# One query projected earlier, the samples' squares in one block, and narrower waits ahead of the up-projection of a hybrid decoder layer

## What is computed

```
h  = rms_norm(x, norm2_g)
q  = rms_norm((h @ w_query).reshape(tokens, 8, 256), qnorm_g)
s1 = q[..., :128] . subkeys[:, 0]      s2 = q[..., 128:] . subkeys[:, 1]
v1, i1 = top_k(s1, 16)                 v2, i2 = top_k(s2, 16)
sc, ci = top_k(v1[:, None] + v2[None, :], 16)      e = (i1 * 128 + i2) at ci
g  = softmax(sc)
a  = gelu(h . u[e])
out = sum over the 8 * 16 chosen experts of g * a * v[e]
```

## Time and profile before

| | before |
|---|---|
| median of 3 runs | 1767.89 us |
| the profiled execution's own time | 1769.0 us |
| its span, from first to last instruction | 1767.2 us |
| PE busy | 1738.9 us (98%) |
| DVE busy | 1202.1 us (68%) |
| ACT busy | 557.6 us (32%) |
| POOL busy | 543.6 us (31%) |
| chain that ended last, by engine | PE 91%, DVE 6%, DMA 1%, issue 1%, ACT 1% |
| the same by line, the largest | L2149 39%, L2197 28%, L1829 17% |

### The profile page before, as it was taken

One profiled execution on the slowest core, in us unless ns is written; L12 is line 12 of the kernel. 1 busy time (PEld: TensorE's weight loads), 2 busy tenths in 40 slices (PEclk: granted clock), 3 DMA queues, 4 the chain that ended last, 5 costly groups with the idle time before them and its releaser, 6 DMA issues.

```text
span 1767.2 us, 30915 instructions
## 1 busy us (share of the span) xinstructions
PE 1738.9 (98%) x12653; PEld 1296.9 (73%) x12653; DVE 1202.1 (68%) x2475; ACT 557.6 (32%) x920; POOL 543.6 (31%) x586
## 2 busy tenths in 40 slices
PE   8999999999999999999999999999989999999999
PEld 7744446788888888888888888888746666666666
DVE  7659866759989948878265555545347667777764
ACT  2013246003242233544344444444212222222220
POOL 0000334022657602000000000000377777777760
PEclk9999999999999999999999999999989999999999
DMA  4431833031223444666998889775589999999991
GB/s 173 111 111 66 294 110 144 4 119 49 87 106 108 155 158 184 247 270 251 323 294 292 302 302 299 255 264 185 224 321 358 361 358 355 353 353 348 351 350 59
DMA packets 137486, 400.00 MB, mean 226 GB/s; under 512 B 13881, under 2 KB 86865, under 8 KB 125569
## 3 DMA queue, kind: packets, MB, share of 16 engines
q1 hardware_dynamic: 108816, 315.81, 48.2%
q0 software_dynamic: 28528, 82.22, 13.2%
HBM read 321.50 MB, written 76.46 MB: 225 GB/s over the span
## 4 chain that ended last, share of the span: by engine, by line
PE 91%; DVE 6%; DMA 1%; issue 1%; ACT 1%; SPq 0%; DVEq 0%; ACTq 0%
PE psum L2149 39%; PE psum L2197 28%; PE psum L1829 17%; PE psum L2170 2%; DMA qrow<-d_q 1%; PE psum L1844 1%; PE psum L2043 0%; PE psum L1964 0%; PE psum L1982 0%; DVE kprod L1239 0%; DVE sSc L1240 0%; PE psum L1881 0%; PE psum L1835 0%; ACT Pb L947 0%; PE psum L1933 0%
## 5 line engine op out<-in xcount | busy, mean ns | idle before, releaser
L2197 PE MATMUL psum<-w_hl,v_hi 128*128 128x376 bf16 x2048 | 493.1, 324 | 4.1 <-issue 4.1
L2149 PE MATMUL psum<-h_hi,u_hi 128*128 128x260 bf16 x2048 | 394.7, 274 | 0.7 <-ACT Ssb L1002 0.7
L2149 PE MATMUL psum<-h_lo,u_hi 128*128 128x260 bf16 x2048 | 394.4, 274 | 0.0
L2149 PE MATMUL psum<-h_hi,u_lo 128*128 128x260 bf16 x2048 | 394.2, 274 | 0.0
L822 POOL DMA_INDIRECT t_dots<-d_acts,t_lists x144 | 171.8, 1193 | 631.8 <-issue 631.8
L2197 PE MATMUL psum<-w_hl,v_lo 128*128 128x376 bf16 x1024 | 332.0, 324 | 3.4 <-issue 3.4
L2197 PEld LDWEIGHTS psum<-w_hl,v_hi 128*128 128x128 bf16 x2048 | 200.9, 98 | 134.5 <-issue 11.3
L1737 DVE TENSOR_TENSOR v_lo<-v_raw,v_hi 128x1024 bf16<-128x1024 f32 x128 | 148.2, 1220 | 133.0 <-issue 86.0
L1039 ACT ACTIVATE v_hi<-v_raw 128x1024 bf16<-128x1024 f32 x128 | 124.7, 1044 | 354.7 <-PE psum L2197 317.1
L1566 DVE TENSOR_TENSOR u_lo<-u_raw,u_hi 128x1024 bf16<-128x1024 f32 x128 | 154.1, 1218 | 121.0 <-ACT u_hi L1010 121.0
L2149 PEld LDWEIGHTS psum<-h_lo,u_hi 128*128 128x128 bf16 x2048 | 198.4, 97 | 31.3
(11 more groups left out here) (414 smaller groups left out, 1780.3 us busy)
## 6 DMA issues: line engine op xcount, KB each, us to landing
u_raw<-in_uT SPq DMA_DIRECT2D x32, 2048.0 KB, 9.1
v_raw<-in_v SPq DMA_DIRECT2D x32, 2048.0 KB
wr<-in_w SPq DMA_DIRECT2D x13, 2048.0 KB, 8.2
d_gate<-stage SPq DMA_DIRECT2D x12, 2048.0 KB, 7.1
w_hl<-d_w SPq DMA_DIRECT2D x32, 768.0 KB
g_up<-d_gate SPq DMA_DIRECT2D x18, 768.0 KB, 9.2
d_w<-w_up SPq DMA_DIRECT2D x18, 768.0 KB, 9.2
d_act<-act_f SPq DMA_DIRECT2D x14, 768.0 KB, 3.9
```

The costliest lines, as they stand in the source:

```text
L2149: mm = pe.matmul(upair[n % 2][:, f, 0:HALF], w[g % 2][:, k, c * P:(c + 1) * P], hs[:, k, halves[f]], start=(k == 0 and x == 0), stop=(k == ...
L2197: mm = pe.matmul(ybank[m][:, 0:DENSE], w[g % 2][:, c, m * P:(m + 1) * P], w_hl[g % WRING][:, z, c, 0:DENSE], start=(g == 0 and c == 0 and ...
```

## The change

It does four things.

1. `queries_before`: the second half of the last head's query, (7, 1), is handled before head 6's scores and no longer before head 7's. PE and ACT both follow this function, and so does the numbering of the PSUM ring.
2. `qzsq` no longer has an axis for the heads. Each head's squares go to columns h, h + 8, ... of one block of 64, all of which are then written, so POOL does not clear it, and PE sums it by 2 products in place of 16.
3. POOL's signal `qz_zero` comes from the clearing of `qz`.
4. `up(0)` waits only until the two blocks in its own banks were taken out, (7, 1) and (7, 2) of the scores, and `up(1)` for the other two, the scores (7, 3) and the samples' unit.

```diff
     if h == 0:
         return [(0, 0), (0, 1)]
-    return ([(1, 0)] if h == 1 else []) + [(h, 1)] + ([(h + 1, 0)] if h + 1 < H else [])
+    if h == H - 1:
+        return []
+    return ([(1, 0)] if h == 1 else []) + [(h, 1), (h + 1, 0)] + ([(H - 1, 1)] if h == H - 2 else [])
...
-    qzsq = put("qzsq", [P, 2, H, 64], F32, D0 + 4096)
+    qzsq = put("qzsq", [P, 2, 64], F32, D0 + 4096)
...
-            pool.memset(qz[:, :, :, :], 0.0)
-            pool.memset(qzsq[:, :, :, :], 0.0).then_inc(qz_zero, 1)
+            pool.memset(qz[:, :, :, :], 0.0).then_inc(qz_zero, 1)
...
-                        A(qzsq[:, a, h, h:64:H], bk[:, HALF - DB:HALF], ACT.Square)
+                        A(qzsq[:, a, h:64:H], bk[:, HALF - DB:HALF], ACT.Square)
...
-            product(bk[0:64, 256:257], [(qzsq[:, a, h, :], ones[:, 0:1]) for a in range(2) for h in range(H)],
+            product(bk[0:64, 256:257], [(qzsq[:, a, :], ones[:, 0:1]) for a in range(2)],
                     ("sc", H, NPT))
...
-            for i in range(NPT - 3, NPT):
-                emptied(pe, ("sc", H - 1, i))
-            emptied(pe, ("sc", H, NPT))
             for n in range(NKEYS):
+                if n == 0:
+                    emptied(pe, ("sc", H - 1, NPT - 3))
+                    emptied(pe, ("sc", H - 1, NPT - 2))
+                elif n == 1:
+                    emptied(pe, ("sc", H - 1, NPT - 1))
+                    emptied(pe, ("sc", H, NPT))
                 up(n)
```

## The result

The changed kernel takes **1773.95 us** (median of 9 executions, 1770.83 to 1776.93) against 1767.89 us (median of 9 on the same chip, 1763.81 to 1769.84): a ratio of 1.0035 with a 95% interval of 1.0027 to 1.0044, or 6.1 us more. The profiled execution took 1771.71 us, with a span of 1769.9 us. The forecast was 1772.3 us, range 1766.8 to 1776.2, slower with 0.72.

What follows compares the result with a forecast made beforehand. PE was taken to bound the kernel, with a gapless DVE deciding the case: late u_lo makes PE 4.3 us late after up(16), taken as +4.4 with the clock. Carried to the median, 1767.89 + 4.4 = 1772.3 us, range 1766.8 to 1776.2.

Steps and rivals of the forecast that it cites:

- What bounds the kernel: PE busy 1738.9 of 1767.2 us; DVE, gapless after its first u_lo, cannot make up a late start.
- Query (7, 1) earlier: Head 7: the 1.16 us wait for squares goes; a wait of about 1.8 us in its scores replaces it.
- the sum: PE's lateness after up(16): +4.3 us, taken as +4.4 with the clock; 1773.4 us for the profiled execution.
- Squares and waits: Ahead of up(0): PE gains 1.7 us from fewer squares products and 0.7 us from the narrower wait.
- u_hi later: Group 0's u_hi 7.07 us later makes DVE late: PE 2.8 us later in up(4), 4.3 us after up(16).
- The wait in up(16): PE waits about 1.5 us for u_lo's third piece in up(16), unless its clock has fallen.
- The clock: PE's wait in up(4) may bring a half-clock stretch costing 1.7 us: the sum +4.5 us, without it +4.3.
- the clock's early fall: Half clock from 523.2 to 526.6, costing 1.7 us; ahead of up(4)'s wait, having or losing it does not count.
- Early gains: Rival: DVE's lateness costs nothing and PE's gains up to up(0) stand, -1.8 to -3.5 us, 1764.4 us; chance 0.07.
- The hidden case: Rival: waits in up(4) and up(16) come out smaller than the slack allows, near no change, 1768 us; chance 0.05.
- The rival of a longer fall of the clock: Two half-clock stretches after up(4)'s waits cost 3.4 us, not 1.7: +6.2 us, 1774.1 us; chance 0.10.
- The down-projection: Rival: its slow start shifts by a third, +- 3.8 us, 1768.5 or 1776.1; 1760.8 if it vanished; chance 0.12.

Runs made afterwards that it cites:

- the second measurement: The changed kernel again, unedited, beside the kernel before on another chip: 1770.76 us against 1766.78, ratio 1.0025.
- the one with u_hi late: The kernel before with u_hi of group 0 issued to ACT behind query (7, 1), PE's order untouched: 1775.88 us, ratio 1.0056.
- the query's move alone: The kernel before with only the new `queries_before`: 1757.93 us against 1752.4, ratio 1.0031.
- the second profile of the kernel before: The kernel before run again without an edit, for its trace on another chip: 1766.75 us, ratio 0.9999.
- the version with u_hi ahead: The changed kernel with u_hi of group 0 made between queries (7, 0) and (7, 1): 1751.19 us against 1752.4, ratio 0.9992.
- The fastest version: The changed kernel with u_hi of group 0 ahead of query (7, 1) and the first two u_lo one round later: 1762.89 us against 1766.78, ratio 0.9978.

## Why the prediction was right

**What bounds the kernel.** Right. The gapless DVE of the earlier trace rows decided the case; its 11.9 us of idleness were forecast as 11.7. One row was misread, and nothing hangs on it: the 1.2 us wait for the squares is the fourth of PE's list and not the second, behind two waits of the trunk (5.4 and 4.3 us).

**Query (7, 1) earlier.** Right: the squares' wait went, and the new one in head 7's scores was 1.40 us against 1.8, inside the bounds of 1.0 and 2.3. That row is one of those that do not add to the sum, as PE waits in up(4) anyway. u_hi was 6.6 us later by the clock of the trace, 7.0 us once the 0.4 us are added by which this execution's trunk was ahead.

**Squares and waits.** Right: 1.98 us became 0.34, and the 0.72 us ahead of up(0) went. Where nobody waits for u_lo, these two are worth 2.4 us in the middle part (forecast for PE alone: 1.7 + 0.7), and the query's move another 1.2 (the 1.16 us wait).

**u_hi later.** Right in its mechanism: waits of 1.1 and 4.64 us in up(4) (forecast 1.4 and 4.7), and none in up(8). Counted from head 5's squares, PE goes on in up(4) at 64.93 us (551.96 - 487.03) and did so at 62.29 us before (549.72 - 487.43): 2.6 us later against the profiled execution, forecast 2.8. The wait in up(16) was to be there "unless the clock has fallen"; the clock fell, and there was none.

**The clock.** This is the term that was mis-sized, twice. First, the prediction had the clock's early fall in the kernel before and said that having it or not did not count. In the changed kernel that is so; in the kernel before it counts, as a part of the slack. The two profiles of the kernel before differ by 1.46 us in the middle part (forecast for such a fall 1.7, but PE worked for only 3.04 of the 3.4 us), and an execution without the fall has only 3.0 and 1.55 us of slack and loses 4.2 us, not 2.8, by the time PE goes on in up(4). Second, the stretch behind the wait cost 2.3 us here and 1.7 us in the other profile. Against the first profile the middle part lost 4.9 us, as 2.6 + 2.3 has it, close to the forecast of +4.4; the medians differ by 6.1 us, which 4.2 + 2.3 would explain if most executions of the kernel before on that chip were without the fall. That is likely, not shown: the 1.1 us between the first profile and the median, which I carried along as a constant, may be the fall or the down-projection, and in the second measurement the medians differ by 4.0 us.

**How near the number was.** The forecast of 1772.3 us is 1.7 us below the median. Part of the nearness of the profiled execution (1771.71 us, the sum gave 1773.4) is luck: it lost 4.9 us in the middle part and was 0.4 us ahead in the trunk and 1.8 us shorter behind the up-projection, which no term of the sum forecast.

**The rivals.** Early gains did not stand: PE waited them away in up(4), and with u_hi as early as before it still waited 1.02 us in up(16). They stand in full only where DVE never idles (3.6 us). The hidden case failed too, since the waits came as the slack allowed. The rival of a longer fall of the clock gave 1774.1 us and came nearest to the median: the half level did last 6.8 us, but 2.2 us of that lay in the wait. The down-projection changed by 1.8 us between the two profiles, half of what that rival allowed, and in the direction of a gain.

## What to carry to other kernels

When a step is moved ahead on one engine, look at what stood behind it there, and for whom: here ACT's conversion for DVE was in the way, and its place was worth some 7 us (5.7 lost or 1.2 gained), six times the 1.16 us of wait that the move removed. What a late producer cost here was its lateness less the consumer's slack at each due point, and a slack read from an execution in which the consumer ran slowly for a moment is too large. The cheap repair is to give the waiting engine other work of its list first: with late u_hi left as it was, two rounds of the ranking ahead of u_lo turned a loss of 0.35% into a gain of 0.09%, and u_hi put back ahead of the last query block with one round made it a gain of 0.22% (each against the kernel before on its own chip).

## What the runs showed of the hardware

**The clock behind a wait.** PE's granted clock fell to 0.50 (the level of 1.2 GHz) in each of the four profiles in which PE stood idle for 3.48 to 4.65 us in up(4), and at none of the waits of up to 1.11 us in up(4) and up(16). It stayed down for 6.8 us in two of them and for 3.4 us in the two others, although the idle time was 4.6 us in three of the four. In the first two it fell while PE still waited, 2.2 and 0.9 us ahead of the wait's end; in the two others PE had been at work again for 0.2 to 0.5 us at full clock. The Trainium skill ("TensorE: Matmul & The Clock Gate", on the HAM clock gate) says that an idle array falls to half rate and comes back only after sustained work. The rows agree for these four waits: the clock came back behind 3.7 to 6.0 us of work without a gap. The price was 1.7 to 3.0 us on top of the wait.

**The fall at 523 comes and goes.** The same list of small products and the same 0.72 us of idling brought a fall in one profile of the kernel before and not in the other. The same rows stand in two more kernels: the one with u_hi late shows the fall (0.51), the query's move alone does not (1.00). So a wait as short as 0.72 us can stand ahead of a fall, and an idle array does not explain it by itself. None of the nine profiles with 4 of these products in place of 32 shows it; the 0.72 us is gone there too, so they do not tell which of the two matters. What decides it stays open.

**The down-projection depends on the chip.** The window of the earlier trace rows in the second profile of the kernel before, and in the version with u_hi ahead, which ran on another chip:

```profile
1286.50:1302.00 15.50, 8.86 (x32) 2.90 (x30) 5.03 (x5) 3.55 (x4) 11.73 (x12) 0.74 0.87 310
```

```profile
1286.50:1302.00 15.50, 15.50 (x99) 9.51 (x98) 13.60 (x14) 4.11 (x6) 12.72 (x10) 1.00 0.89 326
```

32 matmuls against 99 in the same 15.5 us, with much the same DMA traffic. From the last output of the up-projection to the end it is 511.1 us on the one and 496.1 us on the other, and that is the size by which the kernel before took longer on two occasions (1767 us) than on the two others (1752 to 1753 us). The loss does not belong to this one window: the fastest version on the slow chip did 95 matmuls in it and yet took 512.0 us to the end, since it did only 118 between 1370 and 1400 us, where the versions on the fast chips did 190. In the slow case the trace names no releaser, and the clock falls in most of these stretches (0.66 from 1385 to 1400 us there). The cause stays open. Each ratio is taken on one chip, but the stretches vary from execution to execution: the kernel before spreads from 1763.4 to 1771.41 us on the slow chip of the second group and from 1751.62 to 1755.32 us on that of the first, so differences of 1 or 2 us between medians say less on the slow ones.
